# Plain fp32 products in place of split ones in a mixture-of-experts decoder block, with four weight parts loaded earlier

## The reference

```python
y = gelu(s5(u));  val, gate = split(y @ w_glu);  y_ssm = val * sigmoid(gate)      # 512 -> 2 x 1024: the "gated unit"
y_att = sparse_attention(q, k, v, index) @ w_attn_proj
mix = (g_ssm * y_ssm + g_att * y_att) @ w_o                                       # the output projection
h = LN(alpha * h + mix)
# channel mixing: top 4 of 32 experts for each token
hdn = x_e @ w_up[e] + b_up[e]            # 1024 -> 2048
act = (clip(h_lin) + 1) * h_gate * sigmoid(1.702 * h_gate)
y = act @ w_down[e] + b_down[e]          # 1024 -> 1024
h = LN(alpha * h + sum over the chosen experts of gate * y)
```

## Time and profile before

| | |
|---|---|
| median of 3 runs | 1738.14 us (1737.85 to 1738.66) |
| span of the profiled execution | 1738.5 us |
| time of the profiled execution beside its span | none listed apart from the span |
| busy: TensorE, VectorE, ScalarE, GpSimd | 96%, 86%, 61%, 27% |
| device memory read and written | 454 MB and 19 MB, 272 GB/s over the span |

### The profile page before, as it was taken

How to read it: one execution, slowest core, us unless ns; L and a number is a source line. 1 busy time by engine, 2 the same in 40 slices (tenths; PEclk the granted TensorE clock), 3 DMA queues, 4 the chain that set the end, 5 groups by cost and what they waited for, 6 DMA issues and landing times.

```text
span 1738.5 us, 22182 instructions
## 1 busy us (share of the span) xinstructions
PE 1668.7 (96%) x7129; PEld 1088.9 (63%) x7129; DVE 1502.9 (86%) x1689; ACT 1062.2 (61%) x1015; POOL 466.9 (27%) x298
## 2 busy tenths in 40 slices
PE   4999999999998999999999999999999999999996
PEld 2333344466576577777777777777777777777763
DVE  5999886656667899999999999999999999999995
ACT  4323212266444577777777777777777777777771
POOL 4864200074533021122222121212222121211210
PEclk9998999999998999999999999999999999999997
DMA  5111113110407999999999999999999999999973
GB/s 174 49 52 49 49 49 121 49 69 30 142 37 263 375 353 361 361 364 376 366 368 362 372 377 355 370 357 376 368 363 360 373 376 365 365 361 377 378 277 106
DMA packets 91902, 464.76 MB, mean 267 GB/s; under 512 B 21290, under 2 KB 21406, under 8 KB 42617
## 3 DMA queue, kind: packets, MB, share of 16 engines
q1 hardware_dynamic: 80240, 441.67, 66.7%
q0 software_dynamic: 9776, 18.41, 4.3%
q10 hardware_dynamic: 1848, 4.24, 0.7%
HBM read 454.15 MB, written 18.53 MB: 272 GB/s over the span
## 4 chain that ended last, share of the span: by engine, by line
PE 83%; DVE 12%; issue 2%; ACT 1%; DMA 1%; POOL 1%; ACTq 0%; DVEq 0%; POOLq 0%
PE ps L1778 19%; PE ps L1780 19%; PE ps L1779 19%; PE ps L1571 6%; PE ps L1764 3%; DVE w_lo L1205 2%; PE ps L1498 2%; PE ps L1479 2%; PE ps L1493 2%; PE ps L1786 2%; PE ps L1487 1%; PE ps L1680 1%; PE ps L1681 1%; PE ps L1682 1%; DVE scr L1065 1%
## 5 line engine op out<-in xcount | busy, mean ns | idle before, releaser
L1205 DVE TENSOR_TENSOR w_lo<-raw,w_hi 128x2048 fp32r<-128x2048 f32 x384 | 873.7, 2288 | 73.1 <-ACT w_hi L838 71.9
L838 ACT ACTIVATE w_hi<-raw 128x2048 fp32r<-128x2048 f32 x384 | 737.0, 1919 | 239.1 <-PE ps L1780 237.8
L1778 PE MATMUL ps<-w_hi,x_hi 128*96 128x512 f32 x1024 | 414.1, 404 | 0.0
L1780 PE MATMUL ps<-w_lo,x_hi 128*96 128x512 f32 x1024 | 403.0, 394 | 0.0
L1779 PE MATMUL ps<-w_hi,x_lo 128*96 128x512 f32 x1024 | 402.2, 393 | 0.0
L1778 PEld LDWEIGHTS ps<-w_hi,x_hi 128*96 128x96 f32 x1024 | 168.2, 164 | 67.0 <-issue 2.0
L1778 PE MATMUL ps<-w_hi,a_hi 128*96 128x512 f32 x512 | 204.7, 400 | 5.7 <-DVE a_lo L1316 5.7
L1780 PEld LDWEIGHTS ps<-w_lo,x_hi 128*96 128x96 f32 x1024 | 165.3, 161 | 70.8
L1779 PEld LDWEIGHTS ps<-w_hi,x_lo 128*96 128x96 f32 x1024 | 165.9, 162 | 63.9
L605 POOL DMA_INDIRECT gate_now<-gate_rows,row_now x32 | 79.8, 2495 | 455.0 <-DVE tok_out L1346 439.9
L1779 PE MATMUL ps<-w_hi,a_lo 128*96 128x512 f32 x512 | 201.9, 394 | 0.0
(11 more groups left out here) (325 smaller groups left out, 2002.5 us busy)
## 6 DMA issues: line engine op xcount, KB each, us to landing
raw<-in_w_up SPq DMA_DIRECT2D x256, 1024.0 KB, 8.2
raw<-in_w_down SPq DMA_DIRECT2D x128, 1024.0 KB, 10.6
ring<-in_w_in SPq DMA_DIRECT2D x9, 2048.0 KB, 7.8
ring<-in_w_glu SPq DMA_DIRECT2D x4, 1024.0 KB, 6.2
ring<-in_w_o SPq DMA_DIRECT2D x2, 2048.0 KB, 11.7
h<-in_x SPq DMA_DIRECT2D x4, 512.0 KB, 5.6
ring<-in_w_attn_proj SPq DMA_DIRECT2D x1, 2048.0 KB, 8.1
h_rows<-h ACTq DMA_DIRECT2D x4, 512.0 KB
```

The lines of the kernel that those rows point to most:

```text
L838: s.activation(hi_of(c)[:, :], raw_of(c), ACT.Copy).then_inc(s_hi, 1)
L1205: d.tensor_tensor(lo_of(c)[:, :], raw_of(c), hi_of(c)[:, :], ALU.subtract).then_inc(s_lo, 1)
L1778: mm(o, xh, hi_of(c)[:, col], start=start, stop=False)
L1780: return mm(o, xh, lo_of(c)[:, col], start=False, stop=stop)
```

## The change

The split products of the gated unit, the output projection and the experts become plain fp32 products, one instruction each; all the instructions that make halves go. The space of the halves becomes six more buffers: `NRAW` is 12, in an order of places (`PLACES`) such that the first ones are free early. SP loads a part again when TensorE has used it (`s_cu`), not when VectorE has split it. Four of the first weight parts are loaded ahead of the output projection's end: two as soon as the gate tiles are done, two when the attention projection is done, and both ahead of the bias rows in SP's queue; the rest of the first eight and four of the next twelve follow when the projection is done. The load of the slot list moves from SP's queue to GpSimd's. The wait for the count of blocks moves behind the first turn's loads.

```diff
-NRAW, NSPLIT = 6, 4
+NRAW = 12
...
+        PLACES = (4, 5, 2, 3, 0, 1, 6, 7, 8, 9, 10, 11)
...
+            sp.wait_ge(s_tile, tiles_upto[8])
+            for p in range(2):
+                up(-1, p + 4, 0, p)
+            sp.wait_ge(s_tile, tiles_upto[11])
+            for p in range(2, 4):
+                up(-1, p + 4, 0, p)
             sp.wait_ge(s_mix, 8)
...
             sp.wait_ge(s_wo, 2 * TT)
-            for p in range(8):
-                if p >= NRAW:
-                    sp.wait_ge(s_lo, p - NRAW + 1)
+            for p in range(4, 8):
                 up(-1, p + 4, 0, p)
+            for c in range(PARTS):
+                if part_no(0, c) >= NRAW:
+                    sp.wait_ge(s_cu, part_no(0, c) - NRAW + 1)
...
-                    if m == 0:
-                        pe.wait_ge(s_ulo, 1)
-                    pe.wait_ge(s_glulo, m + 1)
...
-                        mm(o[:, :], wglu_hi[:, m % 8, k, :], u_hi[:, k, :], start=k == 0, stop=False)
-                        mm(o[:, :], wglu_hi[:, m % 8, k, :], u_lo[:, k, :], start=False, stop=False)
-                        ins = mm(o[:, :], w_lower[:, k, :], u_hi[:, k, :], start=False, stop=k == 3)
+                        ins = mm(o[:, :], w[:, k, :], uT[:, k, :], start=k == 0, stop=k == 3)
...
-                        mm(o[:, :], mix_hi[:, k, x], wo_hi[r][:, k, :], start=k == 0, stop=False)
-                        mm(o[:, :], mix_hi[:, k, x], wo_lo[r][:, k, :], start=False, stop=False)
-                        ins = mm(o[:, :], mix_lo[:, k, x], wo_hi[r][:, k, :], start=False, stop=k == KD - 1)
+                        ins = mm(o[:, :], mixT[:, k, x], wo_raw[r][:, k, :], start=k == 0, stop=k == KD - 1)
...
-                pe.wait_ge(s_lo, part_no(t, c) + 1)
+                part_in(t, c)
                 for n in range(4):
-                    ins = product(ps[n][0:BLK, :], x_hi[:, p, :], x_lo[:, p, :], c, 512 * n, p == KD - 1)
+                    ins = mm(ps[n][0:BLK, :], xT[:, p, :], raw_of(c)[:, 512 * n:512 * n + 512], start=False,
+                             stop=p == KD - 1)
```

More of the change, by code:

```diff
@@ L222, in over @@
             return nc.alloc_sbuf_tensor_at(name, shape, dt, offset=tensor_at + offset)
[L225 to L231, removed]
         wo_raw = [ring[:, c, :].rearrange("p (k n) -> p k n", k=KD) for c in (0, 3)]
-        wo_lo = [over(f"wo_lo{r}", [P, KD, 512], F32R, at_ring, 4 * c * CHUNK) for r, c in enumerate((0, 3))]
-        wo_hi = [over("wo_hi0", [P, KD, 512], F32R, at_ring, 4 * 2 * CHUNK), over("wo_hi1", [P, KD, 512], F32R, at_u)]
         raw = over("raw", [P, NRAW, PART], F32, at_ring)
[L237 to L241, removed]
+        xT, aT = over("x_T", [P, KD, BLK], F32, at_u), over("a_T", [P, KD, BLK], F32, at_v)
         act_s = far[0:BLK, 0:2, :]
@@ L465, in _ @@
-            sp.wait_ge(s_tr, 2)
-            with sp.Fori(0, final) as i:
-                now = sp.value_load(etab_i[0:1, bass.ds(i, 1)], min_val=0, max_val=NE - 1)
-                later = sp.value_load(etab_i[0:1, bass.ds(i + 1, 1)], min_val=0, max_val=NE - 1)
+            for c in range(PARTS):
+                if part_no(0, c) >= NRAW:
+                    sp.wait_ge(s_cu, part_no(0, c) - NRAW + 1)
+                if c < 8:
+                    up(0, c, 1, c)
+                else:
+                    down(0, c, 0, c - 8)
@@ L470, in _ @@
+            sp.wait_ge(s_tab, 1)
+            final = sp.snap(sp.value_load(etab_i[0:1, NB:NB + 1], min_val=0, max_val=BTAIL - 1) + (NE - 1))
+            turns_left = sp.snap(final - 1)
+            with sp.Fori(0, turns_left) as i:
+                now = sp.value_load(etab_i[0:1, bass.ds(i + 1, 1)], min_val=0, max_val=NE - 1)
+                later = sp.value_load(etab_i[0:1, bass.ds(i + 2, 1)], min_val=0, max_val=NE - 1)
                 for c in range(PARTS):
-                    sp.wait_ge(s_lo, part_no(i, c) - NRAW + 1)
+                    sp.wait_ge(s_cu, i * PARTS + (part_no(1, c) - NRAW + 1))
@@ L472, in _ @@
                     if c < 8:
-                        up(i, c, later, c)
+                        up(i + 1, c, later, c)
                     else:
-                        down(i, c, now, c - 8)
+                        down(i + 1, c, now, c - 8)
             now = sp.value_load(etab_i[0:1, bass.ds(final, 1)], min_val=0, max_val=NE - 1)
             for c in range(4):
-                sp.wait_ge(s_lo, part_no(final, c) - NRAW + 1)
+                sp.wait_ge(s_cu, part_no(final, c) - NRAW + 1)
@@ L953, in _ @@
             for half in range(2):
-                T_hi(a_hi, half, final * 4 + 4 + half, 6 + half)
+                keep_T(aT, half, final * 4 + 4 + half, 6 + half)
             y_back(final, 3)
@@ L1410, in _ @@
                 assert step.n == PER
-            for half in range(2):
-                T_lo(a_lo, a_hi, half, final * 4 + 4 + half, 6 + half)
             next_row(final)
@@ L1799, in down_part @@
                         kk = 2 * p + k
-                        ins = product(ps[4 + r][0:BLK, :], a_hi[:, kk, :], a_lo[:, kk, :], c, DFF * k + 512 * r,
-                                      kk == KD - 1, start=kk == 0)
+                        w = DFF * k + 512 * r
+                        ins = mm(ps[4 + r][0:BLK, :], aT[:, kk, :], raw_of(c)[:, w:w + 512], start=kk == 0,
+                                 stop=kk == KD - 1)
                 ins.then_inc(s_cu, 1)
```

180 lines of the change are left out of this document (40 added, 140 removed).

## The result

The changed kernel takes 2001.3 us in the median of three runs (1998.6, 2001.3 and 2004.3), the kernel before on the same chip 1738.4 us. The ratio is 1.1507, with a 95% interval of 1.1485 to 1.1529: slower by 15%, or by 262 us. A fourth run of 2938 us, at a granted clock of 0.653, is left out here (with it the median is 2002.8 us). A second set of five runs, made beside the experiments, gives 1997.2 to 2002.2 us, 1.1501 [1.1482, 1.1519]. The forecast was 2010 us, with a range of 1994 to 2040. The profiled execution took 1998.64 us, its span is 1996.9.

The account below looks back on a forecast made before the run. TensorE was taken to bound the kernel, the DMA engines just behind. Terms 254.0 + 8.3 + 11.6 - 0.9 + 2.5 - 3.9 = +271.6 on 1738.5, less 0.4, gave 2010 us; range 1995 to 2022, or 1994 to 2040 with contention.

Parts of the forecast that it names:

- The price of a product: On TensorE, a plain fp32 product of 512 columns costs 0.862 us (0.853 to 0.880), dearer by 0.171 than three split matmuls.
- Nothing else in a turn: Expert loop: only dearer products lengthen a turn, to 43.9 us; the DMA engines need 34.6; loop +254.0 us.
- The gated unit: 64 products at +0.171 us give +10.9, less waits of 1.85 and 0.75 us: +8.3, or +9.0 if one stays.
- The output projection: 64 products, each 0.862 instead of 0.680 us: +11.6 us, with the slow-clock piece left as it is.
- The early loads at nothing: Four weight parts loaded ahead cost nothing; eight parts take 22.4 us, and routing already gave the old queue 26 us.
- The biases: Output projection: biases queued behind two weight parts may land some 3 us later, costing nothing, or 3 us without cover.
- Routing and first up part: Before the expert loop: routing -0.9 us without the tokens' lower half; the first expert's up part +2.5 us, 40.1 in all.
- The last down parts: Behind the loop: 16.3 us instead of 20.2, -3.9 with the clock kept, -2 if it falls anyway.
- A, contention: Rival: plain matmuls in the loop pay 1.7% more beside transfers, 0.877 us a product, 2033 us in all; chance 0.17.
- B, a fall of the clock in each turn: Rival: TensorE's clock falls to 1.2 GHz once in each loop turn, +59 us, 2069 in all; chance 0.04.
- C, 0.922: Rival: a plain product in the loop costs four split matmuls, 0.922 us; +100 us, 2110 in all; chance 0.04.
- D, single passes with the transfers as bound: Rival: a product's two records take 0.23 us each, the DMA engines bind at 34.6 us a turn; about 1670; chance 0.03.

## Why the prediction was right, point by point

**The sign and the size** were right: +262 us against +271.9 forecast, inside the range of the likeliest case. Some 10 us of the growth are missing, and the profiled execution lies 13.2 below its forecast.

**The price of a product** is the term that was mis-sized most. I took 0.862 from the gate tiles' 48.28 us for 112 records; the loop pays 0.8585. Over 1488 products the difference is 5.2 us; another 2.5 us are the turn's rest, 43.62 - 48 x 0.8585 = 2.41 us where I left the old 2.49. Of these 7.7 us, 0.7 come back outside the steady turns (31 x 43.62 are 1352.2 of the loop's 1355.0 us, 31 x 35.66 were 1105.5 of 1107.6), and 0.4 are the gather wait that the forecast had already taken off, which leaves the loop's 6.6.

The gate tiles did not pay 0.862 either. Two rows of TensorE's timeline of the kernel before; each begins inside the row of 112 records and runs to its end:

```profile
334.72 16.04 PE L1571 MATMUL ps<-ring 128*128 128x512 f32 x37
...
344.59 6.17 PE L1571 MATMUL ps<-ring 128*128 128x512 f32 x14
```

The starts are 23 records and 9.87 us apart: 0.4291 a record, 0.858 a product. The piece of 48.28 us for 112 records holds, beside this spacing, some 0.1 us at its first start and 0.1 us at its end, and dividing it by the count spreads these over the products. The split matmul had been priced from start to start, the plain one by length over count; from start to start the old trace gave the new price to 0.001 us. The argument that 96 columns of weights cost what 72 and 128 do held: 0.8585 with 96, 0.8584 with 128.

**Nothing else in a turn** held: no wait of TensorE in the loop but 1.7 us at its beginning, DMA share 0.85 against "near 0.8". **The gated unit** was +7.3 against +8.3, of which 64 x 0.0035 = 0.2 is the price; its own run measured the same. TensorE's waits in the stage fell from 5.7 to 2.8 us, by 2.9 where 2.6 were forecast; the rest of the 1.0 us was not traced. **The output projection** was right to 0.2 us like against like, which is the price of its 64 products; the profiled execution happened to lack the slow piece, another -1.7. **The early loads at nothing** held, by the run without them. **The biases** landed later and nobody minded. **Routing and first up part** came out at -1.6 and +2.9, 0.4 under the forecast together. In them executions differ by some 3 us: in a second execution of the changed kernel they took 61.5 us together (537.28 to 598.75), in the profiled one 64.5. **The last down parts** gave -4.0 against -3.9, with the clock kept; the 1.4 us of wait and 13.8 us of products are the forecast's 1.4 and 13.8. The runs with only that part plain show what the forecast's second value, "if the clock falls anyway, -2", was about.

**Not forecast**: the gate tiles end 3.4 us earlier. The point moves from execution to execution: the fourteen profiled ones have it from 347.4 to 351.4 us, and among them the five whose code is the changed kernel's up to there at 347.4, 350.1, 351.3, 349.6 and 351.4. The -3.4 is scatter between executions and no effect of the change, and with the slow piece's -1.7 it makes 5 of the 13.2 us by which the profiled execution is under its forecast.

**The rivals.** A, contention: a product costs 0.8585 in the loop at a DMA share of 0.85 and 0.8584 in the output projection at 0.22; refuted, and so is its premise, as a split matmul costs 0.231 in the gated unit at a share of 0.20. B, a fall of the clock in each turn: the clock is 1.00 over 1354 us; refuted. C, 0.922: refuted for plain products, and exact for four split ones. D, single passes with the transfers as bound: two records of 0.43 us a product; refuted, but the bound it names exists, at 33.3 us a turn and not 34.6 (the run with part of the products left out).

## What to carry to other kernels

Where one engine sets the pace (TensorE, busy 96% of the span), work taken off the others gives nothing back. Three split matmuls, with their splitting on engines that keep up, beat one plain fp32 product here, by 0.167 us on each of the experts' 1536 products. Price the new kind of instruction from a stretch of the old trace where it stands in an unbroken row, from start to start and not by length over count, and multiply with the count of products; even with the coarser price this gave the growth to within 4%. For the last microseconds look at waits behind which the clock falls: behind the loop 3.15 us of idling were followed by slow records that cost 3.0 us in one execution and 1.7 in another, and 1.4 us of idling by none.

## What the runs showed of the hardware

- A plain fp32 product over 512 columns shows as two records of 0.429 us; of each 0.0025 us are not columns (256 columns: 0.2159, 512: 0.4293).
- A split (float32r) matmul of 512 columns takes 0.2304 us in the experts (96 columns of weights, DMA share 0.97), 0.231 in the gated unit (128, 0.20) and 0.2266 in the output projection (128), though half a plain record is 0.2146. Neither the order of operands and banks (a turn of 35.65 us as before) nor a fourth matmul (0.2302, at a share of 0.81) changes it. The cause is open.
- With twelve buffers and 30 of 48 products the transfers reach 393 GB/s (share 1.01); 375 GB/s, worked out from 364 at a share of 0.97, understated what was left.
